# Memory attention in eight units, and mLSTM sample states two sequences at a time

## The reference: what is computed

```python
def memory_attention(qm, g_q_mem, mem_k, mem_v):
    q = rms_norm(qm.reshape(B, L, H_MEM, HD_MEM), g_q_mem)
    s = jnp.einsum('blhd,bmhd->bhlm', q, mem_k) * (HD_MEM ** -0.5)
    p = jax.nn.softmax(s, axis=-1)
    return jnp.einsum('bhlm,bmhd->blhd', p, mem_v).reshape(B, L, D_MEM)

# mLSTM, one chunk, per head: the state C (192 x 192) and the normalizer n (192)
num = einsum('bhts,bshd->bthd', w, v) + einsum('bhed,bthd->bthe', C, q) * w_inter
den = sum(w, -1) + w_inter * einsum('bhd,bthd->bht', n, q)
h = num / maximum(abs(den), exp(-m_t))
C_new = decay * C + einsum('bhs,bshe,bshd->bhed', w_end, v, k)
n_new = decay * n + einsum('bhs,bshd->bhd', w_end, k)
# then a per-head rms_norm of h with a gain, times a sigmoid gate
```

## Time and profile before

| | |
|---|---|
| times of 3 runs | 2698.41, 2704.03, 5250.33 us (median 2704.03) |
| the profiled execution's own time | 2707.99 us |
| its span, first to last instruction | 2706.3 us |
| PE busy | 2585.6 us (96%) |
| PE weight loads busy | 2459.4 us (91%) |
| VectorE (DVE) busy | 1182.1 us (44%) |
| ScalarE (ACT) busy | 810.8 us (30%) |
| GpSimd (POOL) busy | 101.5 us (4%) |
| mean granted TensorE clock | 0.965 of full speed |
| HBM | 206.78 MB read, 12.45 MB written |

### The profile page before, as it was taken

One profiled execution on the slowest core, in us unless ns is written; L12 is line 12 of the kernel. 1 busy time (PEld: TensorE's weight loads), 2 busy tenths in 40 slices (PEclk: granted clock), 3 DMA queues, 4 the chain that ended last, 5 costly groups with the idle time before them and its releaser, 6 DMA issues.

```text
span 2706.3 us, 44423 instructions
## 1 busy us (share of the span) xinstructions
PE 2585.6 (96%) x18995; PEld 2459.4 (91%) x18995; DVE 1182.1 (44%) x1455; ACT 810.8 (30%) x1019; POOL 101.5 (4%) x205
## 2 busy tenths in 40 slices
PE   6999999999988799999999999999998879999998
PEld 6999999999755599999999999999986559999998
DVE  7333335583354334433454343334543734443343
ACT  5222223443122323222233322222334633222222
POOL 1000000000112100000000100000011020000000
PEclk9999999999889789999999999999997989999999
DMA  5222322222212122223222322322232042223222
GB/s 175 82 85 73 91 80 75 62 67 80 60 56 74 61 63 78 74 82 93 72 68 94 115 78 81 87 80 70 89 121 75 26 146 78 78 69 102 78 60 84
DMA packets 334523, 220.74 MB, mean 82 GB/s; under 512 B 11849, under 2 KB 326497, under 8 KB 334420
## 3 DMA queue, kind: packets, MB, share of 16 engines
q1 hardware_dynamic: 325268, 185.83, 23.8%
q0 software_dynamic: 9152, 33.43, 3.8%
HBM read 206.78 MB, written 12.45 MB: 81 GB/s over the span
## 4 chain that ended last, share of the span: by engine, by line
PE 92%; DVE 5%; ACT 1%; issue 1%; DMA 1%; SPq 0%; POOLq 0%; POOL 0%; DVEq 0%; ACTq 0%
PE psum L519 73%; PE psum L545 6%; PE psum L2156 1%; PE psum L1443 1%; PE psum L1502 1%; PE psum L1494 1%; PE psum L1757 1%; PE psum L1483 1%; PE psum L1740 1%; PE psum L2379 1%; PE psum L1474 0%; PE psum L2202 0%; PE psum L1708 0%; PE psum L2185 0%; DMA x_nat<-in_x_sample 0%
## 5 line engine op out<-in xcount | busy, mean ns | idle before, releaser
L519 PE MATMUL psum<-act_hi,whi 128*128 128x288 f32 (+2 forms) x3504 | 756.1, 298 | 12.4 <-DVE act_lo L786 3.8
L519 PE MATMUL psum<-act_hi,wlo 128*128 128x288 f32 (+2 forms) x3504 | 753.8, 297 | 0.0
L519 PE MATMUL psum<-act_lo,whi 128*128 128x288 f32 (+2 forms) x3504 | 753.1, 297 | 0.0
L519 PEld LDWEIGHTS psum<-act_hi,whi 128*128 128x128 f32 (+2 forms) x3504 | 563.7, 188 | 15.3 <-issue 4.9
L519 PEld LDWEIGHTS psum<-act_lo,whi 128*128 128x128 f32 (+2 forms) x3504 | 564.0, 188 | 0.3
L519 PEld LDWEIGHTS psum<-act_hi,wlo 128*128 128x128 f32 (+2 forms) x3504 | 563.4, 187 | 0.4
L498 DVE TENSOR_TENSOR wlo<-raw,whi 128x2048 fp32r<-128x2048 f32 x190 | 435.4, 2292 | 238.7 <-ACT whi L491 238.5
L491 ACT ACTIVATE whi<-raw 128x2048 fp32r<-128x2048 f32 x190 | 362.0, 1905 | 272.6 <-PE psum L519 268.6
L519 PE MATMUL psum<-h_lo,whi 128*128 128x288 f32 x1408 | 301.9, 295 | 0.0
L519 PE MATMUL psum<-h_hi,wlo 128*128 128x288 f32 x1408 | 301.9, 295 | 0.0
L519 PE MATMUL psum<-h_hi,whi 128*128 128x288 f32 x1408 | 301.9, 295 | 0.0
(11 more groups left out here) (410 smaller groups left out, 2143.2 us busy)
## 6 DMA issues: line engine op xcount, KB each, us to landing
raw<-in_w_ffn_up SPq DMA_DIRECT2D x176, 512.0 KB, 5.0
raw<-in_w_ffn_down SPq DMA_DIRECT2D x64, 384.0 KB, 3.9
raw<-in_w_ffn_down SPq DMA_DIRECT2D x64, 320.0 KB, 3.4
raw<-in_w_out SPq DMA_DIRECT2D x16, 512.0 KB, 4.4
raw<-in_w_in_a SPq DMA_DIRECT2D x14, 512.0 KB, 4.7
raw<-in_w_in_a SPq DMA_DIRECT2D x16, 384.0 KB, 4.0
raw<-in_w_kv SPq DMA_DIRECT2D x12, 512.0 KB, 4.1
vpg<-in_cache_v POOLq DMA_DIRECT2D x16, 384.0 KB, 4.0
```

The source lines that it names most:

```text
L519: last = pe.matmul(psum[0:width, 4 * j + 2 * m + h, 0:HALF], w[:, k, cols], a[:, k, h * HALF:(h + 1) * HALF], start=(k == 0 and step == 0) ...
```

## The change

- The sample loop of a head goes by pairs (0, 4), (1, 5), (2, 6), (3, 7). The numerator of one sequence is 32 columns wide instead of 64 and lands in PSUM rows 0 to 31 or 32 to 63; an update takes 32 token rows instead of 64. The two states of a pair are turned into banks 3 and 0, four copies (`turned`) are held instead of two.
- `wv` has a 193rd column (the ones column of v times w_end), so that the second half of the prompt's state update gives the normalizer as row 96; the separate products go.
- In heads 1 to 3 VectorE does the sum of squares, then copies the turned keys, then the rest of the norm of the head before.
- Layer A's query norm uses `query_*`; POOL makes its masks within head 3. Head 3's norm runs late in layer A's attention, as a hook ahead of the copies of the sample outputs.
- The prompt part of the memory attention goes by eight units (a tile of 128 tokens, and the two heads on one half of the array's rows). Four units of weights and turned weights are held, in the idle halves of the weight buffers.
- The sample part: all 16 key and value blocks are loaded ahead (layer A by SP in heads 2 and 3, layer B by POOL); key turns of sequences 0 to 3 stand within the units; turned keys overwrite the loaded ones, copied by ScalarE (0, 1, 4, 5) and VectorE (2, 3, 6, 7); scores of four sequences in a row, in four column strips; outputs in token order, 256 columns for each sequence in its column strip, then a copy, two turns per group, high and low part.

```diff
@@ states_sp, mla_pool @@
         for i in (2 * g, 2 * g + 1):
-            sp.dma_start(carried(i), I["state_C"][0, i % NB, i // NB].rearrange("(e p) d -> p e d", p=DH)) \
+            sp.dma_start(carried(i), I["state_C"][0, sequence_of(i), i // NB].rearrange("(e p) d -> p e d", p=DH)) \
                 .then_inc(state_loaded[g % NG], 16)
+    for head, early in ((3, True), (4, False)):
+        sp.wait_ge(S.k_turned, head)
+        for what, bs in ((0, range(0, 6)), (1, range(1, 7))) if early else ((0, (6, 7)), (1, (0, 7))):
+            for b in bs:
+                memory_load(sp, 0, MA, what, b)
...
     for i in range(HA * NB):
-        h, b = i // NB, i % NB
+        h, b = i // NB, sequence_of(i)
+        if i == (HA - 1) * NB:
+            pool.wait_ge(S.k_turned, HA)
+            query_picks_pool(pool, c)
...
@@ mla_pe @@
+        def turn_state(i):
             pe.wait_ge(state_loaded[i // 2 % NG], 32 * (i // NC + 1))
+            if i >= 2:
+                pe.wait_ge(S.state_turned_copied, i - 1)
+            if i % NB == 1:
+                pe.wait_ge(S.heads_state, h + 1)
             for d in range(2):
                 for e in range(2):
+                    last = pe.transpose(psum[0:DH, 3 - 3 * (i % 2), (2 * d + e) * DH:(2 * d + e + 1) * DH],
                                         carried(i)[:, e, d * DH:(d + 1) * DH], ident[0:DH, 0:DH])
...
         for e in range(2):
+            last_row = DH + e
             for s in range(4):
-                pe.matmul(psum[0:DH, 0, e * DA:(e + 1) * DA], wv[:, s, e * DH:(e + 1) * DH], k_nat[:, s, :],
+                pe.matmul(psum[0:last_row, 0, e * DA:(e + 1) * DA], wv[:, s, e * DH:e * DH + last_row], k_nat[:, s, :],
                           start=(s == 0), stop=(s == 3))
-        for s in range(4):
-            pe.matmul(psum[0:1, 7, 0:DA], cols[:, s, 32 + h:33 + h], k_nat[:, s, :], start=(s == 0), stop=(s == 3))
         pe.matmul(psum[0:NB, 7, DA:2 * DA], w_end_b[:, :], k_nat[0:NSA, 4, :], start=True, stop=True) \
             .then_inc(S.prompt_state, 1)
-        for b in range(NB):
-            i = h * NB + b
-            pe.wait_ge(S.state_turned_copied, i + 1)
+        turn_state(h * NB + 1)
+        for pair in range(NB // 2):
+            i = h * NB + 2 * pair
+            pe.wait_ge(S.state_turned_copied, i + 2)
             for d in range(2):
-                last = pe.matmul(psum[0:NSA, 6, 0:DA + 1], tmp[d][0:DH, b * NSA:(b + 1) * NSA], turned[:, i % 2, d, :],
-                                 start=False, stop=(b == NB - 1 and d == 1), skip_group_check=True)
+                for f in range(2):
+                    last = pe.matmul(psum[32 * f:32 * f + 32, 6, 0:DA + 1],
+                                     tmp[d][0:DH, P * f + 32 * pair:P * f + 32 * pair + 32], turned[:, (i + f) % 4, d, :],
+                                     start=False, stop=(pair == 3 and d == 1), skip_group_check=True)
             last.then_inc(S.num_sample, 1)
-            if b < NB - 1:
-                turn_state(b + 1)
-            if b >= 2:
-                pe.wait_ge(S.state_new, i - 1)
+            if pair < 3:
+                turn_state(i + 2)
+                turn_state(i + 3)
+            if pair:
+                pe.wait_ge(S.state_new, i)
             for e in range(2):
-                last = pe.matmul(psum[0:DH, 1 + b % 2, e * DA:(e + 1) * DA],
-                                 wv_b[0:NSA, b * DA + e * DH:b * DA + (e + 1) * DH], k_nat[0:NSA, 4, :],
-                                 start=True, stop=True)
+                for f in range(2):
+                    at = (pair + 4 * f) * DA + e * DH
+                    rows = slice(32 * f, 32 * f + 32)
+                    last = pe.matmul(psum[0:DH, 1 + f, e * DA:(e + 1) * DA], wv_b[rows, at:at + DH], k_nat[rows, 4, :],
+                                     start=True, stop=True)
             last.then_inc(S.update_ready, 1)
...
@@ mla_act @@
+            if i >= 4:
+                act.wait_ge(S.num_sample, i // 2 - 1)
+            act.activation(turned[:, i % 4, :, DA:DA + 1], n_t[:, :, n:n + 1], ACT.Copy)
+            act.activation(turned[:, i % 4, :, 0:DA], psum[0:DH, 3 - 3 * (i % 2), 0:2 * DA].rearrange("p (d n) -> p d n", d=2),
                            ACT.Copy).then_inc(S.state_turned_copied, 1)
...
@@ mla_dve @@
-        dve.tensor_tensor(wv[:, :, :], v[:, 0:4, 0:DA], w_end[:, 0:4, :].broadcast_to([P, 4, DA]), ALU.mult)
+        dve.tensor_tensor(wv[:, :, :], v[:, 0:4, :], w_end[:, 0:4, :].broadcast_to([P, 4, DA + 1]), ALU.mult)
...
         if h:
-            head_norm_dve(dve, h - 1, c)
+            head_sums_dve(dve, h - 1)
+            dve.wait_ge(S.h_ms, h)
         dve.wait_ge(S.k_turned, h + 1)
         k_psum = flat[:, 0:5 * 256].rearrange("p (t n) -> p t n", n=256)
         dve.tensor_copy(k_nat[:, 0:4, :], k_psum[:, 0:4, 0:DA])
         dve.tensor_copy(k_nat[0:NSA, 4, :], k_psum[0:NSA, 4, 0:DA]).then_inc(S.wv_ready, 1)
+        if h:
+            head_norm_dve(dve, h - 1, c)
...
-        dve.tensor_copy(sumsq[0:1, 0:DA], psum[0:1, 7, 0:DA])
+        dve.tensor_copy(sumsq[0:1, 0:DA], psum[DH:DH + 1, 0, DA:2 * DA])
...
+        for i in range(h * NB, h * NB + NB):
+            last = sequence_of(i) * NS + NS - 1
+            dve.wait_ge(S.update_ready, i // 2 + 1)
             s = carried(i).rearrange("p e d -> p (e d)")
+            dve.scalar_tensor_tensor(s, s, carry[:, last:last + 1], psum[0:DH, 1 + i % 2, 0:2 * DA],
...
@@ mem_attention_pe @@
+    r = u % 2
+    return psum[64 * r:64 * r + 64, 6 + r, 0:256].rearrange("p (x n) -> p x n", x=2)
...
+def mem_attention_pe(pe, l, B):
+    if l == 0:
+        pe.wait_ge(S.state_new, HA * NB)
+        pe.wait_ge(S.heads_state, HA)
+        query_sums_pe(pe, -1, 0)
+        query_spread_pe(pe, -1, 0)
+        pe.wait_ge(S.q_normed, 2)
+        pe.wait_ge(S.h_scaled, HA)
+    else:
+        pe.wait_ge(S.q_normed, 8)
+    def scores(u):
+        t, rows = u // 2, slice(64 * (u % 2), 64 * (u % 2) + 64)
+        if u >= 4:
+            pe.wait_ge(S.ma_exp, 8 * l + u - 3)
+        for x in range(2):
+            last = pe.matmul(mem_scores(u)[:, x, :], B.qn[rows, x, t * P:(t + 1) * P], mk_t[l][rows, x, :],
                              start=True, stop=True)
...
+    def turn(u):
+        pe.wait_ge(S.ma_p, 8 * l + u + 1)
+        if u >= 2:
+            pe.wait_ge(S.ma_pt, 8 * l + u - 1)
+        for y in range(4):
+            last = pe.transpose(psum[:, 4 + u % 2, y * P:(y + 1) * P], ma_e[:, u % 4, y // 2, (y % 2) * P:(y % 2 + 1) * P],
+                                ident[:, :])
+        last.then_inc(S.ma_turned, 1)
+    def outputs(u):
+        pe.wait_ge(S.ma_pt, 8 * l + u + 1)
+        if u >= 2:
+            pe.wait_ge(S.ma_out_lo, 10 * l + u - 1)
+        for x in range(2):
+            for m in range(2):
+                h = 2 * x + u % 2
+                last = pe.matmul(mem_mix(u)[:, x, :], mv[l][:, m, h * DM:(h + 1) * DM], ma_pt[:, u % 4, 2 * x + m, :],
+                                 start=(m == 0), stop=(m == 1))
+        last.then_inc(S.ma_out, 1)
+    def turn_keys(b):
+        if b == 0:
+            pe.wait_ge((S.mem_cache_a, S.mem_cache_b)[l], 256)
+        if b < 4:
+            pe.wait_ge(S.ma_exp, 8 * l + 5 + b)
+        elif b < 6:
+            pe.wait_ge(S.ms_kt, 4 * l + b - 3)
+        else:
+            pe.wait_ge(S.ms_kt_dve, 4 * l + b - 5)
...
+    def sample_scores(g):
+        pe.wait_ge(S.ms_kt, 4 * l + 2 * g + 2)
+        pe.wait_ge(S.ms_kt_dve, 4 * l + 2 * g + 2)
+        pe.wait_ge(S.ms_qz, l + 1)
+        pe.wait_ge(S.ma_pt, 8 * l + 7 + g)
+        for pair in range(2):
+            for x in range(4):
+                last = pe.matmul(psum[32 * x:32 * x + 32, 4 + g, 0:M], B.qz[:, pair, 4 * g + x, :],
+                                 keys_turned(B, 4 * g + x)[:, pair, :], start=(pair == 0), stop=(pair == 1),
+                                 skip_group_check=True)
+        last.then_inc(S.ms_scores, 1)
...
+    def sample_outputs(g):
+        pe.wait_ge(S.ms_pt, 2 * l + g + 1)
+        pe.wait_ge(S.ma_out_lo, 10 * l + 7 + g)
+        for m in range(2):
+            for x in range(4):
+                last = pe.matmul(psum[32 * x:32 * x + 32, 6 + g, 0:M], ma_pt[:, g, m, 32 * x:32 * x + 32],
+                                 B.vs[:, 4 * g + x, m, :], start=(m == 0), stop=(m == 1), skip_group_check=True)
+        last.then_inc(S.ms_out, 1)
...
+    for u in range(4):
+        scores(u)
     if l:
         query_sums_pe(pe, 3, 1)
         query_spread_pe(pe, 3, 1)
         pe.wait_ge(S.q_normed, 10)
+    turn(0)
+    for u in range(8):
+        if u + 1 < 8:
+            turn(u + 1)
+        if u + 4 < 8:
+            scores(u + 4)
+        if u == 4:
+            turn_keys(0)
+            turn_keys(1)
+        if u == 6:
+            turn_keys(2)
+            turn_keys(3)
+        outputs(u)
+    sample_scores(0)
+    for b in range(4, 8):
+        turn_keys(b)
+    sample_scores(1)
     for g in range(2):
```

(93 more changed lines are left out.)

416 lines of the change are left out of this document (145 added, 271 removed).

## The result

| | before | after |
|---|---|---|
| median | 2703.57 us (15 runs) | 2716.62 us (15 runs, 2708.87 to 2721.89) |
| ratio after to before | | 1.0042, 95% interval 1.0026 to 1.0058 |
| the profiled execution, its span | 2707.99, 2706.3 us | 2720.51, 2718.9 us |
| mean granted clock | 0.965 | 0.949 |

The forecast was 2677, between 2656 and 2708. The change made the kernel slower by 0.4%, and the time lies outside the range. That it stays within 2% was right; sign and size were not. One run of before took 5250.33; its other fourteen lie between 2692.29 and 2715.01.

What follows compares the result with a forecast made beforehand. TensorE was taken as the bound (92% of the span; barely in the sample loops), a ring across engines in the memory attention. Heads -23.0, layer A -7.3, layer B +3.5 gave -26.8: 2677 us on the median, range 2656 to 2708.

Steps and rivals of the forecast that it cites:

- the new wait: Head of each mLSTM sample loop: TensorE waits for VectorE to empty the prompt state's bank; +2.6 us per head, +10.4.
- Pairs, -19.6: mLSTM sample loops: two sequences at a time, 2.85 us per pair, loop 12.15 instead of 17.06; -19.6 us for four heads.
- Rival 2: mLSTM sample loops: the strips run one behind the other, the pairs gain 14 us less, total 2691; chance 0.15.
- Normalizer, key copy, L1483, norm: mLSTM heads: separate products gone -5.6, earlier key copy -7.1, faster matmuls after a shorter wait -2.3, late head norm +1.2 us.
- Queries of A: Layer A's memory attention: new query norm, first scores at 883.3, first maximum 10 us earlier.
- Eight units: Prompt part of both memory attentions: half-tile units at 4.4 us each, 8.8 per tile against the old 5.0.
- The ring: Memory attention units: turn, scores, outputs, high part, low part, weights wait on each other; 4.4 us, 6.5 at half clock.
- slow cycles: Memory attention units: two cycles at half clock taken in each layer, +4.2 us each.
- rival 1: Both memory attentions: half clock through all units, A's end +8.2 and B's +21.8 us, total 2711; chance 0.2.
- Sample part: Sample part of the memory attentions, after the last output: 16.5 us in A, 15.1 in B.
- Sum: All edited stretches: mLSTM heads -23.0, layer A's attention -7.3, layer B's +3.5, together -26.8 us.
- Moves of DMAs: Cache loads and query masks moved to other queues or earlier: no cost; uncovered, each late load costs a few us once.

Runs made afterwards that it cites:

- wide: The changed kernel with numerators 64 columns wide and updates 64 rows deep, pairs and the new wait kept: 2762.62 us, ratio 1.0213.
- wait_before: The kernel before with one wait added: each head's first numerator waits until VectorE has emptied the prompt state's bank; 2734.61 us, ratio 1.0084.
- bank2: The changed kernel with each head's second state turned into bank 2 ahead of the prompt's state, so without the new wait; 2675.83 us, ratio 0.9886.
- m_nopairs: The kernel before with only the normalizer row and the earlier key copy, sequences still one by one; 2690.22 us, ratio 0.9949.
- b2_warm: bank2 with unused products of 224 columns where TensorE waits in the query norm and the units; 2652.71 us, ratio 0.9802.

## Why the prediction was wrong, point by point

**The step that failed** is the price of the new wait: "+2.6 per head ... nothing hides it". Its length was right (1.76 and 0.67 of idleness after, with the turn between them), but it was charged for itself alone. It also halves the clock of the loop behind it and of the next head's start. Taking it out saved 41 us instead of 10. In the prediction the clock is priced with the attentions and with L1483, never with the new wait; the heads had been at 1.00 in every loop, and I took that for a property of the loop. The prediction even put L1483's 4.52 instead of 2.84 down to PE's wait of 3.91 ahead of it, and did not ask the same of the wait that it added. wide and wait_before show that the same loop runs at either clock.

**Pairs, -19.6.** The mechanism was right: 2.45 per pair at full clock in bank2 against 2.85, loop 11.24 against 12.15. Strips do run at once: the numerators of a pair take 0.78, the lower bound (0.80) that I did not take, and its updates 0.88. By the Trainium skill (TensorEngine Tiling (Array Packing), Theoretical Speedup) up to 2x was to be had for a dimension of at most 64; the trace agrees, 0.78 for what takes 1.60 one sequence after the other. Rival 2 is refuted. In the kernel as changed, with 4.41 per pair, the gain was not there.

**Normalizer, key copy, L1483, norm: -5.6 -7.1 -2.3 +1.2, together -13.8.** m_nopairs gave -12.5 (between -20.5 and -6.8). The sum fits; one term was too small, as L1483 takes 2.84 in all heads of m_nopairs and after, where heads 1 to 3 before took 4.37 to 4.52: -4.8, not -2.3. The key copy fits (waits of 2.28, 3.90 and 3.91 became 1.04). The late norm was not tried by itself.

**Queries of A.** First maximum at 885.63, forecast 883.3: head 3 had ended 1.7 later, and the first scores took 2.1 (883.52 to 885.63) instead of 1.6.

**Eight units.** The ring was read rightly: 4.4 at full clock (4.44 and 4.59 in b2_warm), 6.5 at half (6.73 to 6.87 after). The number of slow cycles was wrong: two were taken for each layer, and nearly all were slow. The rows at 1.00 in the earlier trace rows (55% and 68% busy), of which the first stood against rival 1, do not carry over: the units of A after were busy for 30.93 of 45.20, 68% as well, and stood at 0.50. How much PE worked in a stretch did not tell which clock it got.

**Sample part.** 16.5 forecast for A, 15.7 measured (933.1 to 948.8).

**Sum.** Heads +2.4 instead of -23.0; layer A +0.5 instead of -7.3 (from the squares to what follows the attention, 71.9 against 71.4); layer B +9.3 instead of +3.5. Rival 1's total, 2711, came near 2716.6 but for half of the reason, and so by luck: it priced the clock in the attentions (A +8.2 and B +21.8, too much) and left the heads their gain. That one mechanism acts in three places did not stand among the cases, and so the range ended too low.

**Moves of DMAs.** No wait for one of the moved loads shows in the rows read; their effect by itself was not tried.

## What to carry to other kernels

Price a wait of TensorE by the clock behind it, not by its length: a new wait of 2.4 us ahead of a loop cost 10 us per head, of which filling it with useless products gave back more than half, and turning one tile into a bank that happened to be free all. Before granting a loop the clock of its old profile, ask what PE does just ahead of it, and look for a free buffer or a later eviction that closes the gap.

## What was not expected of the hardware

- A busy engine need not get the clock back: 23.00 of 23.00 us busy at 0.50 in wait_before, 21.36 of 21.36 in the kernel after, most of it matmuls that use 64 or 96 rows. The loop's same instructions ran at 1.00 in 16.00 of 16.00 in wait_before's next head, and in that head L1483 did get the clock back within 4.4 us.
- A wait of 1.22 us was enough for a fall in two heads of four, and not in the other two.
- Unused work made the kernel faster: 2643.06 to 2623.82.
- Four column strips run fully at once: sixteen instructions of 256 columns in 1.07, where four take 1.05 in the earlier trace rows.
